# Bias rows spread from a copy in DRAM, the decay table asked for earlier, and the modulation's sums as rows of 32 output partitions

## What is computed

```python
# first block
h = x + hybrid_mixer(rms_norm(x, norm1_g), w_in, conv_w, conv_norm_g, ret_norm_g, w_out)
#   the mixer: 4 groups of 128 conv channels, 4 retention heads of 128 (rotary q and k,
#   scores times a decay table, group norm, times silu of a gate), side by side times w_out
h = h + jnp.square(relu(rms_norm(h, norm2_g) @ w_up)) @ w_down          # w_up 1024 x 4096
x = rms_norm(h, final_norm_g)
# second block
ada = c @ w_ada + b_ada                                                # w_ada 1024 x 6144
shift1, scale1, gate1, shift2, scale2, gate2 = split(ada, 6)
proj = (rms_norm(x, g_norm1) * (1 + scale1) + shift1) @ w_in            # q, k, v, gates, indexer
#   8 heads of forgetting attention and 8 heads of attention over the 256 keys that an
#   indexer picks; the latter's logits get a bias rel_bias[bucket(t - s)] for each head
x = x + gate1 * (merged @ w_out)
h2 = rms_norm(x, g_norm2) * (1 + scale2) + shift2
x = x + gate2 * (jnp.square(relu(h2 @ w_mlp1)) @ w_mlp2)
return rms_norm(x, g_final)
```

## Time and profile before

| | |
|---|---|
| three executions | 1390.11, 1390.27, 1386.93 us; median 1390.11 |
| profiled execution | 1390.86 us, of it the span 1389.1 |
| mean granted clock of PE over the span | 0.991 |
| busy share: PE, DVE, POOL, ACT | 98, 59, 41, 37% |
| largest groups on PE | L551, 984 units' matmuls of each of the three terms, 385 to 397 us each |
| moved by DMA | 156.68 MB, 113 GB/s in the mean |

### The profile page before, as it was taken

The page is one execution under the profiler, slowest core; times in us unless marked ns, Lnnn a source line. Parts: engine busy times, 40 slices in busy tenths (PEclk is TensorE's granted clock), DMA queues, the critical chain, the costliest instruction groups (busy, mean ns, idle before and its releaser), DMA issues.

```text
span 1389.1 us, 18486 instructions
## 1 busy us (share of the span) xinstructions
PE 1361.6 (98%) x6394; PEld 1108.3 (80%) x6398; DVE 816.7 (59%) x1082; ACT 517.7 (37%) x818; POOL 562.8 (41%) x230
## 2 busy tenths in 40 slices
PE   8998999999999999999999999999999999999997
PEld 6787878888888888887777777888878888888886
DVE  5463568484766847885988866334554343352474
ACT  5333234331322314234356665323345323142233
POOL 4323335353562646324322223443524535345361
PEclk9999999999999999989999999999999999999999
DMA  7454235365473754713522233333422423323221
GB/s 222 117 89 98 76 106 159 98 178 157 143 227 99 210 167 112 212 34 106 77 77 63 75 92 83 100 91 91 141 72 93 134 77 109 88 89 119 79 91 60
DMA packets 213252, 156.68 MB, mean 113 GB/s; under 512 B 8996, under 2 KB 193696, under 8 KB 213064
## 3 DMA queue, kind: packets, MB, share of 16 engines
q1 hardware_dynamic: 212728, 154.62, 39.9%
q10 hardware_dynamic: 464, 1.27, 0.3%
HBM read 151.13 MB, written 4.74 MB: 112 GB/s over the span
## 4 chain that ended last, share of the span: by engine, by line
PE 50%; DVE 2%; ACT 1%; issue 0%; POOL 0%; ACTq 0%; DVEq 0%
PE ps L551 28%; PE ps L1020 12%; PE ps L969 3%; PE ps L908 2%; PE ps L885 1%; PE ps L872 1%; PE ps L858 1%; PE ps L859 1%; DVE work L2082 1%; DVE work L2079 0%; DVE work L2064 0%; PE ps L862 0%; DVE top L2062 0%; DVE sel L2067 0%; POOL w_lo L514 0%
## 5 line engine op out<-in xcount | busy, mean ns | idle before, releaser
L514 POOL TENSOR_TENSOR w_lo<-raw,w_hi 128x1024 fp32r<-128x1024 f32 x222 | 559.3, 2527 | 792.9 <-ACT w_hi L1067 792.6
L551 PE MATMUL ps<-u_hi,w_hi 128*128 128x512 f32 x984 | 396.5, 403 | 4.0 <-POOL w_lo L514 2.3
L551 PE MATMUL ps<-u_hi,w_lo 128*128 128x512 f32 x984 | 385.6, 392 | 0.0
L551 PE MATMUL ps<-u_lo,w_hi 128*128 128x512 f32 x984 | 385.4, 392 | 0.0
L1067 ACT ACTIVATE w_hi<-raw 128x1024 fp32r<-128x1024 f32 x222 | 233.0, 1054 | 283.5 <-PE ps L1020 91.0
L551 PEld LDWEIGHTS ps<-u_hi,w_hi 128*128 128x128 f32 x984 | 187.0, 190 | 43.0 <-POOL w_lo L514 4.3
L551 PEld LDWEIGHTS ps<-u_hi,w_lo 128*128 128x128 f32 x984 | 185.9, 189 | 39.9
L551 PEld LDWEIGHTS ps<-u_lo,w_hi 128*128 128x128 f32 x984 | 186.3, 189 | 36.8 <-issue 1.0
L551 PE MATMUL ps<-y_hi,w_hi 128*128 128x512 f32 x320 | 126.7, 396 | 0.1
L551 PE MATMUL ps<-y_hi,w_lo 128*128 128x512 f32 x320 | 124.6, 389 | 0.0
L551 PE MATMUL ps<-y_lo,w_hi 128*128 128x512 f32 x320 | 124.6, 389 | 0.0
(11 more groups left out here) (270 smaller groups left out, 1826.6 us busy)
## 6 DMA issues: line engine op xcount, KB each, us to landing
raw<-w_in SPq DMA_DIRECT2D x69, 512.0 KB, 3.9
raw<-w_mlp SPq DMA_DIRECT2D x64, 512.0 KB, 3.9
adaw<-w_ada SPq DMA_DIRECT2D x32, 768.0 KB, 4.6
raw<-w_up SPq DMA_DIRECT2D x32, 512.0 KB, 5.9
raw<-w_down SPq DMA_DIRECT2D x32, 512.0 KB, 6.6
raw<-w_out SPq DMA_DIRECT2D x16, 512.0 KB, 4.1
bias_rows<-fbrow SPq DMA_DIRECT2D x4, 640.0 KB
xtok<-x SPq DMA_DIRECT2D x4, 512.0 KB, 7.6
```

The lines of the kernel that those rows point to most:

```text
L514: pool.tensor_tensor(w_lo[:, s, :], raw[:, s, :], w_hi[:, s, :], ALU.subtract).then_inc(lo_ready[s], 1)
L551: last = pe.matmul(ps[0:cols, bank, :], w[:, s, c], r[:, k, :], start=(k == ks[0] and w is w_hi and r is r_hi), stop=(k == ks[-1] and w is ...
```

## The change

1. **Bias rows.** One copy writes the first row of each head (`brow_copy`, 8x640, behind the loads of retention pass 1). Four `brow_spread(j)` copy, in DRAM, the first row of heads 2j and 2j+1 to their 127 others (2x127x640). Spread 0 follows the retention loads, spread 1 the conv loads, spread 2 the w_out loads, spread 3 the wait for `ada_sum`, and the value loads wait for its landing.
2. **Decay table.** Its DMA moves from ACT's queue to SP's, behind the loads of pass 0. DVE's wait for it moves behind both rotations of head 0.
3. **Start.** ACT makes `first_half(0)` ahead of the wait for the gain and of the first u_hi.
4. **w_ada.** Each load and each `ada_piece` is two places earlier; the first two stand in `wout`, whose second pass of loads now waits for the end of the mixer. DVE's loops over the halves of a quarter are unrolled. Its wait for `brow_out` moves to the head of `wout`.
5. **The sums.** PE makes each as a row of 512 columns: 12 matmuls in place of 48, four at a time, with `pick` (a column of ones among zeros, 32 wide) as weights, into output partitions 32g to 32g+31 (`ada_rows`, L822). ACT copies the bank to `adaw` (`ada_row_copy`), and PE turns it with four transposes for each half (`ada_turned`, L831). `ada_sum` counts to 4, the last behind units 0 and 1 of the indexer.
6. **High parts first.** `two_units_early` (L859, L860, L863) takes the place of `two_units` behind n3 and n4: the two terms with u_hi wait for u_hi, the third for u_lo. `last_rows` stands behind it.
7. vrow, oneh and rbias lie over the area of sdec.

```diff
         ccs = sb("ccs", [P, T], where=mix)
         qf, kf = sb("qf", [P, T], where=mix), sb("kf", [P, T], where=mix)
+        pre = ExitStack()
+        vrow = sb("vrow", [NVEC, P], where=pre)
+        oneh = sb("oneh", [BUCKETS, NREL], where=pre)
+        rbias = sb("rbias", [BUCKETS, HEADS], where=pre)
+        pre.close()
         sdec = sb("sdec", [P, NT, T], where=mix)
...
+        gones, pick = sb("gones", [P, 2], where=one), sb("pick", [P, 64], where=one)
...
                 for s, at in enumerate([W1_RQ, W1_RK, W1_RG]):
                     load(st_ret, s, j, (whole, cols(w_in, at + j * P)))
-            def brow_copies(j):
+            def brow_copy():
                 sp.wait_ge(sem("brow_read"), 2)
-                sp.dma_start(bias_rows[:, ds(j * (P // NQ), P // NQ), :],
-                             bass.AP(fbrow[:].tensor, fbrow[:].offset, [fbrow[:].ap[0], [0, P // NQ], [1, NREL]])
+                sp.dma_start(bias_rows[:, 0:1, :],
+                             bass.AP(fbrow[:].tensor, fbrow[:].offset, [fbrow[:].ap[0], [0, 1], [1, NREL]])
+                             ).then_inc(sem("brow_out"), 16)
+            def brow_spread(j):
+                if j == 0:
+                    sp.wait_ge(sem("brow_out"), 16)
+                h = 2 * j * P * NREL
+                sp.dma_start(bass.AP(bias_rows.tensor, h + NREL, [[P * NREL, 2], [NREL, P - 1], [1, NREL]]),
+                             bass.AP(bias_rows.tensor, h, [[P * NREL, 2], [0, P - 1], [1, NREL]])
                              ).then_inc(sem("brow_out"), 16)
             def value_rows(s, k0, k1, done):
             sp.dma_start(rope[:], tab[:, TAT["cos"]:TAT["cos"] + 2 * T].rearrange("p (a t) -> p a t", a=2)
                           ).then_inc(sem("rope_in"), 16)
             ret_loads(0)
-            with sp.Fori(1, NQ) as j:
+            sp.dma_start(decay[:], tab[:, TAT["decay"]:TAT["decay"] + NQ * T].rearrange("p (a t) -> p a t", a=NQ)
+                         ).then_inc(sem("decay_in"), 16)
+            ret_loads(1)
+            brow_copy()
+            with sp.Fori(2, NQ) as j:
                 ret_loads(j)
-                brow_copies(j - 1)
-            brow_copies(NQ - 1)
+            brow_spread(0)
             with sp.Fori(0, NQ) as j:
...
+            def ada_load(q, d, i, b):
+                sp.wait_ge(sem(f"ada_used{b}"), q * 4 + 2 * d + i + 1)
+                src = w_ada_2.rearrange("(q k p) n -> q k p n", q=NF, p=P)[
+                    ds(q, 1), d, :, ds(i * 3 * D + b * 3 * D // 2, 3 * D // 2)]
+                sp.dma_start(adaw[:, b, :], src.rearrange("q p n -> p (q n)")).then_inc(sem(f"ada_in{b}"), 16)
...
+            brow_spread(1)
+            for i in range(KC // 4):
...
+                    if i == 1 and s == 1:
+                        sp.wait_ge(sem("mix_done"), 1)
+                    if i == 1 and s % 2:
+                        ada_load(0, 0, 0, s // 2)
+            brow_spread(2)
+            def quarter(q, last=False):
+                for i in range(2):
+                    for s in range(4):
+                        load(st_mlp, s, q * 4 + i, (whole, cols(w_up, q * D + i * 4 * P + s * P)))
+                        if s % 2:
+                            ada_load(q, i, 1 - i, s // 2)
+                for i in range(2):
+                    for s in range(4):
+                        src = w_down.rearrange("(q k p) n -> q p k n", q=NF, p=P)[
...
                  (lambda d: d[:, :, HD:HD + HEADS], cols(w_in_2, W2_F, HEADS)),
                  (lambda d: d[:, :, HD + 32:HD + 32 + IDX_HEADS], cols(w_in_2, W2_WI, IDX_HEADS)))
-            sp.wait_ge(sem("ada_sum"), 2)
-            sp.wait_ge(sem("brow_out"), 16 * NQ)
+            sp.wait_ge(sem("ada_sum"), 4)
+            brow_spread(3)
+            sp.wait_ge(sem("brow_out"), 16 * (NQ + 1))
             def value_loads(r, at):
...
             mlp_down(st_mlp, "mlp", NF - 1, 0)
-            def ada_columns(m0, m1, done=False):
-                for m in range(m0, m1):
-                    last = pe.matmul(ps[:, (SB, OU)[m // (3 * KC)], m:m + 1], acc[:, m * P:(m + 1) * P], ones[:, 0:1],
-                                     start=True, stop=True)
-                if done:
+            def ada_rows(n, at, opens=True, closes=True):
+                for g in range(4):
+                    j = 4 * n + g
+                    last = pe.matmul(ps[32 * g:32 * g + 32, SB, :], pick[:, 32 - at:64 - at], acc[:, j * QW:(j + 1) * QW],
+                                     start=opens, stop=closes)
+                if closes:
                     last.then_inc(sem("ada_sum"), 1)
-            def with_columns(s, m0, done):
-                pe.wait_ge(sem("acc_done"), 2 * (NF * 4 - 1) + m0 // 12)
+            def ada_turned(half):
+                pe.wait_ge(sem("arow_ready"), half + 1)
+                for b in range(4):
+                    last = pe.transpose(ps[:, (OU, TR)[half], b * P:(b + 1) * P], adaw[:, half, b * P:(b + 1) * P], ident)
+                last.then_inc(sem("ada_sum"), 1)
+            pe.wait_ge(sem("acc_done"), PIECES - 1)
+            pe.wait_ge(sem("squares"), 7)
+            ada_rows(0, 0)
+            for s in range(4):
+                unit(st_mlp, s, NF * 4 - 1, y_hi, y_lo)
+                if s == 0:
+                    ada_turned(0)
+            both_sums()
+            pe.wait_ge(sem("acc_done"), PIECES + 1)
+            ada_rows(1, 0, closes=False)
+            roots_turned(0)
+            ada_rows(2, 1, opens=False)
+            roots_turned(1)
+            def two_units_early(st, i, name):
                 for k in range(KC):
-                    unit(st_mlp, s, NF * 4 - 1, y_hi, y_lo, part=(k, k + 1), opens=(k == 0), closes=(k == KC - 1))
-                    if k >= 2:
-                        ada_columns(m0 + 2 * (k - 2), m0 + 2 * (k - 1), done and k == KC - 1)
-            with_columns(0, 0, False)
-            with_columns(1, 12, True)
-            unit(st_mlp, 2, NF * 4 - 1, y_hi, y_lo)
-            with_columns(3, 24, False)
-            both_sums()
-            pe.wait_ge(sem("acc_done"), 2 * NF * 4 + 1)
-            ada_columns(36, 42)
-            roots_turned()
-            ada_columns(42, 48, True)
...
             turn_row(3, 1, 1)
-            mlp_up(st_mlp2, "n4", 0, 0, last_rows)
+            two_units_early(st_mlp2, 0, "n4")
+            last_rows()
+            for s in range(2, 4):
+                unit(st_mlp2, s, 0, u_hi, u_lo)
             mlp_up(st_mlp2, "n4", 0, 1)
             for r in range(2):
                 down_rows(0, r)
...
                 act.activation(xrow[:, i, c * QW:(c + 1) * QW], ps[:, bank, :], ACT.Copy).then_inc(sem("xrow_ready"), 1)
+            def ada_row_copy(half):
+                act.wait_ge(sem("ada_sum"), 2 * half + 1)
+                act.activation(adaw[:, half, 0:QW], ps[:, SB, :], ACT.Copy).then_inc(sem("arow_ready"), 1)
...
+            first_half(0)
             act.wait_ge(sem("gain_ready"), 1)
             for m in range(KC):
                 act.wait_ge(sem("x_ready"), m + 1)
                 act.activation(u_hi[:, m, :], xres[:, m, :], ACT.Copy,
                                scale=vec[:, VAT["norm1_g"] + m:VAT["norm1_g"] + m + 1]).then_inc(sem("norm_hi"), 1)
-                if m < 2:
-                    first_half(m)
+                if m == 0:
+                    first_half(1)
                 if m % 2 and m // 2 + 1 < SLOTS:
                     cast(st_rv, m // 2 + 1, 0)
             cast(st_ret, 0, 0)
...
             dve.wait_ge(sem("rope_r"), 2)
-            dve.wait_ge(sem("decay_in"), 16)
             dve.wait_ge(sem("vec_ready"), 1)
...
             rotate(0, 0, qf)
             rotate(1, 0, kf)
+            dve.wait_ge(sem("decay_in"), 16)
             ret_decay(0)
...
+                        if gained and i == 1 and s % 2:
+                            ada_piece(0, 0, 0, s // 2)
+            dve.wait_ge(sem("brow_out"), 16)
```

More of the change, by code:

```diff
@@ L426, in _ @@
-            mlp(st_mlp, w_up, w_down, True)
+                    if i == 1 and s == 1:
[12 more added lines that the diff above has]
+                        src = w_down.rearrange("(q k p) n -> q p k n", q=NF, p=P)[
+                            ds(q, 1), :, :, ds(i * 4 * P + s * P, P)].rearrange("q p k n -> p (q k) n")
+                        load(st_mlp, s, q * 4 + 2 + i, (whole, src))
+                        if s % 2 and not (last and i == 1):
+                            ada_load(q + i, 1 - i, 1 - i, s // 2)
@@ new lines, in _ @@
+            both_sums()
[5 more added lines that the diff above has]
+            def two_units_early(st, i, name):
+                for k in range(KC):
+                    c = slice(k * P, (k + 1) * P)
+                    pe.wait_ge(sem("norm_hi"), before(name) + k + 1)
+                    for s in range(2):
+                        if k == 0:
+                            pe.wait_ge(lo_ready[s], st.turn(s, i) + 1)
+                            wait(pe, bank_free[s], st.turn(s, i))
```

(33 more changed lines are left out.)

179 lines of the change are left out of this document (70 added, 109 removed).

## The result

| | before | changed |
|---|---|---|
| median of 8 executions | 1389.26 us (1386.93 to 1390.75) | 1393.91 us (1392.84 to 1396.05) |
| ratio | | 1.0036, 95% interval 1.0026 to 1.0047 |
| profiled execution, span | 1390.86, 1389.1 us | 1393.41, 1391.6 us |
| PE busy | 1361.6 us | 1351.2 us |

The change costs 4.7 us (3.6 to 6.5 by the interval), 2.5 by the two profiled executions: that of before happens to lie 1.6 above its median. The sign was right, the size was not: 29.6 had been forecast. The time lies just under the forecast's own range of 1395 to 1457.

What follows compares the result with a forecast made beforehand. TensorE, busy 1361.6 of 1389.1 us, was taken as the bound. From 1390.9, small gains less 0.5 for transposes gave -20.3, spreads 1 to 3 +8.4, +12.4 and +29.1: 1420; own range 1395 to 1457, stated range with rivals 1378 to 1455.

Steps and rivals of the forecast that it cites:

- (a): Start: ACT rounds the first weights before the first u_hi, shortening TensorE's 1.3 us wait: -0.6 us.
- (b): Decay table's wait moved behind both rotations: ret_scores' wait and the low clock behind it go, -3.9 us.
- (c): ret_turn's 3.58 us wait, laid to the bias copies in the DMA queue, goes with its half clock: -6.6 us.
- X: Duration of one DRAM-to-DRAM bias-row spread on two DMA engines: 22 us taken, bounds 15.5 and 50.
- Spreads 1 and 2: Weight loads queued behind these copies delay the last conv sum and the first w_up unit: +8.4 and +12.4 us.
- Spread 3: SP's chain of ada_sum, spread, landing and value loads delays the values: X + 4.1 and low clock 3, +29.1 us.
- rival 4: Whole kernel: X near 13, gains and losses cancel, 1391 us; chance 0.08.
- (d): MLP units: 36 one-column modulation columns give way to four 512-column matmuls and four transposes, net -6.8 us.
- (e): Norm gap before the second block: rows replace 12 columns, TensorE starts sooner, some half clock goes: -2.2 us.
- rival 2: In the modulation sums, the 32-partition groups run one after the other instead of overlapping: 1434 us; chance 0.15.
- (f): Behind the second norm, high parts first shortens the 1.73 us wait for the first u_lo: -0.7 us.

Runs made afterwards that it cites:

- b1: On the kernel before, only DVE's wait for the decay table moved behind the two rotations, its DMA left on ACT's queue: 1385.32 us (0.9981).
- e4: On the changed kernel, only the bias rows undone, four SBUF copies at their old places and no spreads: 1380.69 us (0.993).
- e8: On the changed kernel, each spread's two loops swapped, 127 rows outermost and 2 heads inside: 1437.07 us (1.0357).
- e1: On the changed kernel, spread 3 issued ahead of SP's wait for ada_sum, no longer behind it: 1377.17 us (0.9912).
- e2: On the changed kernel, each spread writes 32 rows (31 in the first) of all 8 heads, same bytes: 1384.01 us (0.996).
- e3: On the changed kernel, the transposes of the first half of the sums one down unit later: 1392.92 us (1.0031).
- e12: On the changed kernel, e1 and e2 together, spreads over 8 heads and the last ahead of the wait for ada_sum: 1376.40 us (0.9917).
- e9: On e1, one-column products replace the 512-column rows in the norm gap, second-half sums left out: 1380.05 us (0.9944).
- e5: On e1, index units 0 and 1 in the old order, all three terms behind u_lo: 1376.87 us (0.9925).

## Why the prediction was right and wrong

**Start, decay table, ret_turn (a, b, c).** Together right: -11.1 forecast, the lead at the last conv sum is 10.6. It is made of (b) and (c). Behind the scores of head 0 the lead is 4.1 (the first ret_turn starts at 71.21 for 75.30; forecast 3.9), and (c) adds 6.5 (forecast 6.6). The ret_turn of the earlier trace rows, called the first there, is the third of four. Their witnesses are b1 for (b), and for (c) e4, where the old copies bring ACT's 11.5 us and ret_turn's 3.6 back. The price of the half clock behind ret_turn varies: e4 paid less than the kernel before. Of (a) nothing is shown. The first matmul with weights starts at 7.65 for 8.29, 0.18 of it because the first load landed earlier, but by 13.36 for 13.41 the lead is down to 0.05:

```profile
13.36 0.39 PE L695 MATMUL ps<-w_hi,u_hi 128*128 128x512 f32 x1
```

In the experiments that have this edit the same matmul starts anywhere from 12.87 to 14.37; what sets it there was not looked into.

**X.** This is the step that failed: "so I stay near the fast end but below it, as both sides are DRAM: 15 GB/s, **X = 22**". That both sides are DRAM was taken as a reason for a slower engine, and no row showed it. X measured 12.9. An engine that both reads and writes DRAM moved 25 to 26 GB/s in three shapes (1, 2 and 8 engines), more than the 21 of a weight load, so X lay outside the bounds of 15.5 and 50 on the fast side. The weight loads' 21 were no upper bound: their packets are shorter (512 bytes a row of 128 columns, 2560 here). That this is the cause was not tried. The figure of the Trainium skill (DMA: Bandwidth & Descriptors, "Latency and other measured facts"), 207 GB/s at a row pitch of 512 KiB, gives an estimate of 13 an engine if it is divided by 16, and was further off still; the measurement decides. The prediction put the sum "some 14 us higher" by it; its own terms give 9, three microseconds at each of spreads 1 to 3.

**Spreads 1 and 2.** Forecast +8.4 and +12.4, measured 0 and about 1: the lead is 10.6 at the first w_up unit (245.04 to 234.41) and 9.6 where the last four down units begin (575.91 to 566.31). The mechanism was right and X alone wrong: with X = 26 (e8) the two cost 10.9 and 9.8, by how that run's lag behind the changed kernel grows: 5.4 at the first conv sum, 16.3 at the last, 26.1 at the first w_up unit.

**Spread 3.** Forecast X + 4.1 and 3 of low clock, 29.1. With the measured X that is 20.0; measured were 15.0 + 1.4. By the chain, X + 10.1 behind two_units (614.45) gives 637.4, measured 636.81. TensorE's own need came 1.4 later than written, since the transposes and the wait for the third weights took 1.7 where 0.5 stood. e1 and e2 show the chain from both ends.

With X = 12.9 and all else as written the sum gives about 1391, which is **rival 4** as it stood in the text (X near 13, gains and losses cancel), at a chance of 0.08. That rival stood for a change of less than 4 us; the 4.7 measured lie at its edge. So the right sign is luck: at the true X the forecast's own terms cancel, and what made the kernel slower was a term that the prediction had sized wrongly, (d), against (e) and spread 3, which came out cheaper. Three smaller terms make up the rest:

- (d) forecast -6.8, measured -0.9 (lead 9.6 to 10.5). The products' price was right (four groups of 32 partitions, 8 passes, take 0.99 us, 566.31 to 567.30, forecast 1.0; they overlap, rival 2 falls), and 36 columns were 8.4 us (30.2 for the four units with them, 21.8 without; forecast 8.3). But the sum has no term for a wait of TensorE for ACT's copy of the row; of the product's sums the text says only that they "stay off its path", VectorE's, "and I cost that at nothing". That wait is 2.9 us, since ACT does a square and a cast first; behind it 2.4 go in half clock, and the rest for draining and the transposes. The last four down units begin and end, in the kernel before, with the starts of these rows:

```profile
575.91 0.40 PE L551 MATMUL ps<-y_hi,w_hi 128*128 128x512 f32 x1
...
606.09 0.36 PE L575 MATMUL ps<-ones,nt 128*128 128x1 f32 x2
```

In the changed kernel the stretch runs from the row at 566.31, shown above, to this one:

```profile
595.57 0.28 PE L596 MATMUL ps<-ones,nt 128*128 128x1 f32 x2
```

  e3 showed that DVE caught up during this wait: taken away alone, on the changed kernel, it bought 1 us; with modulation(0) moved too, on e12, 3.0.
- (e) forecast -2.2, measured -5.0: the gap is 2.1 shorter (9.96 to 7.89), and the half clock from 616 to 622 goes whole (2.9) where I had taken 1.1. e9 confirms the reason named, the rows, for the 2.9; the 2.1 are partly chance, since the gap varies from profile to profile (see e5 and e9).
- (f) forecast -0.7, measured -0.8 by this wait: TensorE waits 0.92 for u_hi, where it waited 1.7 for u_lo.

## What to carry to other kernels

Before a DMA is reshaped, look for the largest number up to 16 that divides its outermost dimension: the same 650 KB took 26, 13 or 3.3 us with 1, 2 or 8 engines. A copy with no hurry belongs ahead of the queue's next wait, not behind it; one swapped line was worth 16.7 us. And when a wait of the bound engine is taken away, look at which engine was catching up in it.
